# Second MLP product of an encoder layer: twenty block products over a 3 x 4 x 2 split in place of seven half products over a 2 x 2 x 2 split

## The reference, cut to what matters

```
h  = rms_norm(x, g_mlp) * (1.0 + scale2) + shift2     # (1536, 1024)
ff = square(relu(h @ w_ff1)) @ w_ff2                   # (1536,4096), then (1536,1024)
x  = x + gate2 * ff
y  = rms_norm(x, g_final)
```

## Time and profile before

| | |
|---|---|
| median of three runs | 1447.25 us (1443.58 to 1447.31) |
| span of the profiled execution | 1441.9 us |
| what lies around that span in the runs shown | 1.7 to 5.4 us, 5.35 to the median |
| TensorE busy | 1402.4 us, 97% of the span |
| VectorE, ScalarE, GpSimd busy | 809.9, 591.7, 479.5 us |
| first product, from its first matmul | 477.3 us |
| second product | 958.27 us to 1430.64 us |

### The profile page before, as it was taken

How to read it: one execution, slowest core, us unless ns; L and a number is a source line. 1 busy time by engine, 2 the same in 40 slices (tenths; PEclk the granted TensorE clock), 3 DMA queues, 4 the chain that set the end, 5 groups by cost and what they waited for, 6 DMA issues and landing times.

```text
span 1441.9 us, 18527 instructions
## 1 busy us (share of the span) xinstructions
PE 1402.4 (97%) x7594; PEld 1188.8 (82%) x7594; DVE 809.9 (56%) x756; ACT 591.7 (41%) x709; POOL 479.5 (33%) x275
## 2 busy tenths in 40 slices
PE   4999999999999989999999999999999999999997
PEld 2777777888888778888888888888888888888886
DVE  5967668794338994444453345352756433344575
ACT  6667888566135532232222222232232222433241
POOL 0011111137002655474545555432232222232131
PEclk9999999999999999999999999999999999999998
DMA  9344311203602234343334333479997444445542
GB/s 371 152 153 170 135 61 37 73 23 95 234 0 88 88 125 160 114 154 114 122 143 145 119 119 126 172 258 389 391 384 297 146 146 146 161 177 204 204 160 88
DMA packets 75411, 232.35 MB, mean 161 GB/s; under 512 B 5696, under 2 KB 9920, under 8 KB 66368
## 3 DMA queue, kind: packets, MB, share of 16 engines
q1 hardware_dynamic: 75328, 231.17, 43.5%
HBM read 166.14 MB, written 65.01 MB: 160 GB/s over the span
## 4 chain that ended last, share of the span: by engine, by line
PE 50%; issue 3%; POOL 1%; DVE 1%; ACT 0%; POOLq 0%; ACTq 0%
PE bank L981 17%; PE bank L982 17%; PE bank L983 16%; POOL w_lo L2339 1%; DVE x L2151 0%; DVE w_raw L2102 0%; POOL x L2361 0%; ACT hin_hi L1527 0%; ACT w_hi L1515 0%; DVE x L2123 0%; POOL w_s L2315 0%; PE bank L1038 0%; POOL w_lo L2331 0%; PE bank L1031 0%; POOLq L2369 0%
## 5 line engine op out<-in xcount | busy, mean ns | idle before, releaser
L981 PE MATMUL bank<-hin_hi,w_lo 128*128 128x512 f32 (+1 forms) x896 | 302.4, 337 | 1.4 <-DVE hin_lo L2107 1.4
L982 PE MATMUL bank<-hin_lo,w_hi 128*128 128x512 f32 (+1 forms) x896 | 301.7, 337 | 0.0
L983 PE MATMUL bank<-hin_hi,w_hi 128*128 128x512 f32 (+1 forms) x896 | 301.1, 336 | 0.0
L2107 DVE TENSOR_TENSOR hin_lo<-hin,hin_hi 128x3072 fp32r<-128x3072 f32 x28 | 140.9, 5031 | 209.1 <-ACT hin_hi L1527 209.1
L2339 POOL TENSOR_TENSOR w_lo<-w_raw,w_hi 128x2048 fp32r<-128x2048 f32 x28 | 129.6, 4628 | 329.9 <-ACT w_hi L1515 328.4
L981 PEld LDWEIGHTS bank<-hin_hi,w_lo 128*128 128x128 f32 x896 | 170.1, 190 | 20.4 <-issue 2.3
L983 PEld LDWEIGHTS bank<-hin_hi,w_hi 128*128 128x128 f32 x896 | 169.9, 190 | 18.0
L982 PEld LDWEIGHTS bank<-hin_lo,w_hi 128*128 128x128 f32 x896 | 170.1, 190 | 17.7 <-issue 0.2
L1515 ACT ACTIVATE w_hi<-w_raw 128x2048 fp32r<-128x2048 f32 x28 | 53.6, 1916 | 287.6 <-PE bank L983 181.7
L2331 POOL TENSOR_TENSOR w_lo<-w_raw,w_hi 128x512 fp32r<-128x512 f32 x51 | 73.5, 1441 | 208.5 <-ACT w_hi L1461 208.5
L1470 ACT ACTIVATE hid<-bank 128x768 f32<-128x768 f32 (+2 forms) x68 | 52.5, 772 | 162.7 <-PE bank L983 155.3
(11 more groups left out here) (273 smaller groups left out, 3171.1 us busy)
## 6 DMA issues: line engine op xcount, KB each, us to landing
hin<-hid_all SPq DMA_DIRECT2D x28, 1536.0 KB, 6.6
hid_all<-hid SPq DMA_DIRECT2D x105, 384.0 KB, 2.5
w_raw<-in_w_ff SPq DMA_DIRECT2D x36, 1024.0 KB, 8.9
w_raw<-in_w_ff SPq DMA_DIRECT2D x68, 256.0 KB, 2.9
mod_raw<-in_w_mod SPq DMA_DIRECT2D x16, 1024.0 KB, 5.1
x<-in_xT SPq DMA_DIRECT2D x5, 2048.0 KB, 14.1
w_sums<-w_raw SPq DMA_DIRECT2D x8, 1024.0 KB, 15.3
w_raw<-w_sums SPq DMA_DIRECT2D x8, 1024.0 KB, 10.1
```

Of the source, the lines that this page charges most:

```text
L981: pe.matmul(out, w_lo, v_hi, start=first, stop=False, skip_group_check=True)
L982: pe.matmul(out, w_hi, v_lo, start=False, stop=False, skip_group_check=True)
L983: return pe.matmul(out, w_hi, v_hi, start=False, stop=last, skip_group_check=True)
L2107: dve.tensor_tensor(hin_lo[n % 3][:].rearrange("p t n -> p (t n)"), hin[n % 3][:].rearrange("p t n -> p (t n)"), hin_hi[n % 3][:].rearrang ...
```

## The change

The second product is cut into 3 token blocks of 512, 4 inner blocks of 1024 and 2 column blocks of 512 (24 block products), and is computed as 20 products of sums of blocks. An inner block of 1024 has eight 128-wide tiles; the kernel goes through all 20 products for the first four tiles of each block (steps 0 to 19), then through all 20 for the other four (steps 20 to 39). A step has 4 banks x 4 tiles x 3 = 48 matmuls of 512 columns. Each product's result goes, with a sign, into one or more of six output blocks.

- The products alternate between two sets of four banks at first (indices 0 to 10 in `SEQ`); from index 11 on several follow one another on the same set: 17, 16, 13, 18, 15 on banks 0 to 3 and 12, 14, 11, 0 on banks 4 to 7 (the numbers are names of products).
- The splits into high and low are done in two pieces of 128 x 1024. The high parts have two buffers. In steps of `BY_BANK` a bank is finished before the next is begun, and both pieces are freed only at the step's end.
- VectorE makes 17 weight sums of 128 x 2048 in each half (34 in all) and 8 token sums of 128 x 2048 in each half; 13 additions of a whole output block (4 banks) from PSUM in the first half and 19 in the second. ScalarE copies 5 blocks from PSUM and one block within SBUF. `conv_block`, new, turns the accumulated sum into `gate * sum + x` for each of the six blocks in the second half; from then on additions carry the gate.
- The first product stores nine forms of 128 x 512 a job (fewer in the two parts of job 0): six combinations of 512 columns in place of four of 768. The four hidden blocks stay in one tensor `hidq`; ScalarE's copies into it wait for the combinations of the job before that read the same rows. Two blocks of job 0 are read back from DRAM before job 5 ends (`reload_rest`).
- The residual is loaded block by block late in the second half. Squares are added on GpSimd (`fin_adds`).

TensorE, order and waits (cut):

```
+SEQ = (7, 6, 10, 9, 5, 2, 8, 3, 4, 19, 1, 17, 16, 13, 18, 15, 12, 14, 11, 0)
+BY_BANK = (0,) + tuple(range(11, NP))
+SAME_NEXT = (11, 12, 13, 14, 16, 17, 18)
+        def bank_emptied(n, b):
+            if b % 2:
+                return
+            m = same_bank(n)
...
+            if added(m):
+                pe.wait_ge(ff2_add, adds_to(m, b // 2))
+        def product(n):
+            if n % NP in BY_BANK:
+                split_in(n, 0)
+                split_in(n, 1)
+                for b in range(4):
+                    bank_emptied(n, b)
+                    m = bank_part(n, b, range(GF))
...
+                    if n == NS - 2 and b == 1:
+                        fin_spread(0)
...
+            for p in range(2):
+                split_in(n, p)
+                for b in range(4):
+                    if p == 0:
+                        bank_emptied(n, b)
+                    m = bank_part(n, b, (2 * p, 2 * p + 1))
```

VectorE, order of the second product:

```
+        for s in range(NS):
+            h, i = half_of(s)
+            if i == 8:
+                token_add(h, "a14")
+            if s > 0 and added_later(s - 1):
+                block_adds(s - 1, 1)
+            if s + 1 < NS:
+                tok_split_lo(s + 1, 0)
+            if s > 0 and not added_later(s - 1):
+                block_adds(s - 1, 0)
+                block_adds(s - 1, 1)
+            if s + 1 < NS:
+                tok_split_lo(s + 1, 1)
+            for name in {1: ("b0a",), 2: ("b0b", "v"), 3: ("b2", "b3"), 5: ("b19",), 6: ("b4",), 7: ("b1",), 8: ("b17",),
+                         11: ("b13",), 13: ("v15", "b12"), 14: ("b14a", "b14b"), 16: ("b11",)}.get(i, ()):
+                weight_sum(h, name)
+            if s == NP - 1:
+                weight_sum(1, "u")
+                weight_sum(1, "b6")
+            if i in (8, 9, 10, 11, 12, 14, 16):
+                token_add(h, {8: "a1", 9: "a17", 10: "a16", 11: "a13", 12: "a18", 14: "a12", 16: "a11"}[i])
+            if h and i in CONV_AT:
+                conv_block(CONV_AT[i])
+            if s == NS - 2:
+                fin_diagonal(0)
+            if s < NS - 1 and added_later(s):
+                block_adds(s, 0)
+            if s == NS - 2:
+                for v, k in ((1, 0), (1, 1), (1, 2), (1, 3), (0, 0)):
+                    final_tile(0, v, k)
```

`block_adds(n, e)` adds banks 2e and 2e + 1 of product n to its output block or blocks; `added_later(s)` holds for `SAME_NEXT` and for step 19. GpSimd:

```
+        for s in range(NS):
+            if s + 1 < NS:
+                w2_split_lo(s + 1, 0)
+                w2_split_lo(s + 1, 1)
+            if s == NP + 16:
+                fin_adds(0, (1, 0), (1, 1))
+            elif s == NP + 18:
+                fin_adds(1, (2, 1), (2, 0))
+                fin_tiles(0, (1, 0))
```

SyncE, what it does at job 5, ahead of the next weights:

```
+        def reload_rest():
+            sp.wait_ge(hid_step, hid_at(REST, FR))
+            sp.wait_ge(st_hid[0], stored(0, REST))
+            sp.wait_ge(st_hid[1], stored(1, REST))
+            sp.wait_ge(st_keep, 16)
+            sp.dma_start(hidq[:, H11, 0:CH], keep_d).then_inc(ld_keep, 16)
+            sp.dma_start(hidq[:, H21, 0:CH], hid_d[0, 0, :, 0]).then_inc(ld_keep, 16)
```

More of the change, by code:

```diff
@@ L80 @@
[L80 to L92, removed]
+H11, H12, H21, H22 = range(4)
+G5, G2, G3, G15, GZ, G19 = range(6)
+G7, G6, GR, G9, G0, G4 = range(6)
+NST = 9
+FORMS = ("a00", 10, 5, 3, 2, 15, "a10", 19, "z", "a22", "a02", 7, "r", 6, 9, 8, 4, 0)
@@ new lines, in kind_of, with steps_of, hid_at, stores_of @@
+def kind_of(q):
+    return JOBS[q][0] % 8 // GF
+def steps_of(q):
+    both = (U2, C11, B11, C22, B22, C12, B12)
+    _, c0, c1 = JOBS[q]
+    if c0:
+        return both + (F19, FZ)
+    if c1 == CH:
+        return both + (F3, F5, F2, F15)
+    return both + ((F0, F4, F7, F6, F9, FR) if kind_of(q) else (F3, F19, F5, FZ, F2, F15))
+def hid_at(q, step):
+    return sum(len(steps_of(i)) for i in range(q)) + steps_of(q).index(step) + 1
+def stores_of(q):
+    _, c0, c1 = JOBS[q]
+    return (7, 8) if c0 else range(7) if c1 == CH else range(NST)
@@ new lines, in added, with copied, adds_to, copies_to @@
+def added(n):
+    h, i = half_of(n)
+    return ADDED[h].get(SEQ[i], ())
+def copied(n):
+    return COPIED.get(SEQ[n], ()) if n < NP else ()
+def adds_to(n, e):
+    return 2 * sum(len(added(m)) for m in range(n)) + (e + 1) * len(added(n))
+def copies_to(n):
+    return sum(len(copied(m)) for m in range(n + 1)) + (n >= SEQ.index(9))
+def same_bank(n):
+    side = SEQ[n % NP] in RIGHT
+    return next((m for m in range(n - 1, -1, -1) if (SEQ[m % NP] in RIGHT) == side and (added(m) or copied(m))), None)
@@ L306, in build_encoder @@
[L306 to L312, removed]
-    fin_acc = place("fin_acc", [P, HTOK], F32, hid_at + 12288)
@@ new lines, in _ @@
+        for n in range(NS):
+            if n == NS - 2:
+                fin_columns(0)
+            product(n)
+        pe.wait_ge(fin_last_added, 3)
+        for b in range(4):
+            pe.matmul(bank[3][:, 8 + b:9 + b], sq[0, 0][:, 0, b * P:(b + 1) * P], ones[:, 0:1], start=(b == 0),
+                      stop=False, skip_group_check=True)
+        pe.wait_ge(fin_last_sqd, 4)
+        for b in range(4):
+            m = pe.matmul(bank[3][:, 8 + b:9 + b], sq[0, 1][:, 3, b * P:(b + 1) * P], ones[:, 0:1], start=False,
+                          stop=True, skip_group_check=True)
@@ L2050, in out_of, with halves, split, pieces @@
                 return ps[:, 2 * CH * buf + c0:2 * CH * buf + c1]
-            slot, at = hid, NHID * q
+            def halves(lo_row):
+                return hidq[:, lo_row:lo_row + 2, CH:HTOK]
+            def split(i):
+                return form[i][:].rearrange("p (a b) -> p a b", a=2)
+            def pieces(row):
+                return hidq[:, row, 0:CH].rearrange("p (a b) -> p a b", a=2)
+            def stored_before(j):
+                if q:
+                    after(dve, st_hid[j], stored(j, q - 1))
+            h11, h12, h21, h22 = (hidq[:, i, 0:CH] for i in range(4))
             if step == U2:
@@ L2183, in _ @@
         token_lo(P5, 1)
-        for step in (B22, C12, B12, T1):
+        for step in (B22, C12, B12, F3):
             hid_out(0, step)
@@ L2194, in _ @@
         token_lo(P4, 1)
-        hid_out(0, T4)
+        for step in (F2, F15):
+            hid_out(0, step)
         for q in range(1, NJ):
```

1191 lines of the change are left out of this document (740 added, 451 removed), and 5 rows, old and new, of the table ADDED.

## The result

| | before | after |
|---|---|---|
| median | 1446.01 us (1443.58 to 1447.31, 4 runs) | 1502.31 us (1500.18 to 1504.36, 4 runs) |
| ratio, 95% interval | | 1.039 [1.037, 1.041] |
| span of the profiled execution | 1441.9 us | 1502.4 us |
| second product | 472.4 us | 509.9 us |
| behind its last matmul | 11.3 us | 15.8 us |

A forecast was written before the change was run, and what follows sets the result against it. It took TensorE's matmuls to bound the second product; 434.7 us of columns, 3 of small matmuls and 60 of waits made that stage 25.3 us longer. With +2 first product and +2.6 tail: 1477 us, range 1435 to 1500.

The forecast's parts named there:

- the walk: Second product, step by step through the engines' queues: TensorE waits 14 us in the first half, 46 in the second.
- 30.3 us of columns are saved: Second product: 1920 matmuls of 512 columns take 434.7 us in place of 465.0; a step shrinks to 10.87 us.
- VectorE and GpSimd hold each other: Second product: VectorE's SBUF work stands still during GpSimd's 4.8 us a step; instructions with one operand in PSUM aren't held.
- Waits of 60 us in the second product: New TensorE waits, mostly on VectorE: 60 us, at least 21 or 10 from below, about 85 from above.
- Indices 0 to 10: Second product, both halves: products change banks each time, so an addition has a whole step; waits taken as 0.
- The clock stays at full: Second product: no loss to half clock in the sum, since VectorE is behind and a slower step is partly covered.
- rival 3: Second product: clock falls after some six waits of 8 us or nearly, 16 us, 1493 us; chance 0.13, 0.05 with late loads.
- First product +2 us: First product: reload holding SyncE at job 5 ahead of job 6's weights costs 2 us, range 0 to 6.
- At the job boundary 0: First product: ScalarE's copy waits for the sum of H11 and H21, ready before the copy is due; 0 us.
- Tail +2.6: After the second product's last bank: 14 us in place of 11.3, so +2.6 us, range 0 to 5.
- Rival 1: Second product: splits fit, matmuls still bound, GpSimd's holds fall under PSUM additions or idle time; 10 us waits, 1427 us; chance 0.20.

The follow-up runs named there:

- e1: Changed kernel with GpSimd's low weight pieces of the second product written as zeros instead of subtracted, their product left out: 1458.97 us, ratio 1.009 to the kernel before.
- e9: Changed kernel with GpSimd writing zeros three times for each low weight piece of the second product, as long as the subtraction took: 1457.8 us, ratio 1.008.
- e10: e5 with the second product's low weight subtractions, all but the first step's, moved from GpSimd to VectorE, nothing left out: 1464.92 us, ratio 1.013.
- e2: Changed kernel with VectorE's addition of banks 0 and 1 moved ahead of the step's sums: 1484.64 us, ratio 1.027.
- e3: Changed kernel, first product: job 0's sum of H11 and H21 ahead of token sums, job 6's first two weight loads ahead of late stores and reload: 1496.26 us.
- e5: Changed kernel with the reorders of e2 and e3, and the first diagonal's product after bank 3 of step 38 instead of bank 1: 1477.29 us, ratio 1.022.
- e7: e5 with GpSimd writing zeros for the second product's low weight pieces as in e1: 1446.29 us, ratio 1.001.

## Why the prediction was right or wrong

The direction and the mechanism came out as forecast; the size did not. The time lies 25 us above the forecast of 1477 us. Two terms of the sum that stood at nothing or nearly so account for most of it. The half clock around TensorE's waits was put at 0 and cost some 16 us. The first product was put at +2 us, with 0 at its job boundary, and cost 13.5. The waits themselves were 9 us fewer than the walk had.

- *30.3 us of columns are saved: right.* A step without a wait takes 10.87 us; the one shown above is 10.90 us long.
- *VectorE and GpSimd hold each other: right, and it is the cause.* e1 and e9 show it without GpSimd's reads, e10 with the same subtraction on VectorE. What was read from the earlier trace rows before is what the new kernel does: 2.4 us where 1.2 would do. PSUM additions aren't held: 1.21 us. The held ones suffer in both directions. GpSimd's piece takes 2.97 us in the mean where I took 2.4. The sums of squares take 6.7 us where I took 4.6.
- *Waits of 60 us in the second product: near.* 51.3 us. First half 14 forecast, 15.9 measured, at the indices named (11: 4.9; 13: 2.8; 14: 2.3; 16: 2.9; 19: 3.0). Second half 46 forecast, 32.8 measured at the same indices (forecast in brackets): 11: 5.9 (4); 13: 9.6 (10.8); 14: 0.8 (8.4); 16: 3.4 (8); 17: 2.0 (2.7); 18: 9.5 (11); 19: 1.6 (1). Index 14 failed because I let each step begin afresh. A TensorE that has just stood for 9.6 us, and then runs at half clock, has given VectorE the time to catch up. e2 fits this: there index 13 waits for nothing, and index 14's step is 7.6 us too long. Indices 0 to 10: 2.7 us for 0, over both halves.
- *The clock stays at full: wrong, and the largest error of the sum.* I had it as rival 3 at 16 us and 18%, and left it out "partly covered". It cost 15.7 us in the second product, counted from TensorE's busy time at half clock, and at most 20.4 with all that the waits and the small matmuls leave over. Four waits of the second product and two of the first are above 4 us, and the granted clock fell during all six; it also fell with some of 2.0 to 3.4 us, and with others of 2.3 and 2.8 us it did not. The two stretches of one step show 2.9 us lost behind 4.9 us of wait. The rival's size was near (16 us in all; 2.7 us per wait against 2.0 in the mean of eight falls). Its condition was wrong: 8 us or longer lay far above the 1 us of idle time that had kept the clock in the earlier trace rows. I had no row between the two, though the trace had one: the wait of 2.5 us at about 506 us, with the clock at full behind it. The Trainium skill (TensorE: Matmul & The Clock Gate, What's actually happening) speaks of half clock after idling and of recovery under sustained work. The trace agrees, and a wait of 2.0 us was enough in one place. (The end of the trace before, which the prediction called on, shows the fall alone. The return is in the two stretches above, 0.79 and then 1.00.)
- *First product +2 us: wrong, +13.5 in the profile.* "At the job boundary 0" failed. I priced the copy's new wait from VectorE's work in a steady job, and not from job 0, where the token sums lie ahead of the form. At job 5 I counted GpSimd's wait for the weights. I missed that ScalarE has that split and TensorE's copy in one queue. e3 gives back 3.1 us of it in the profile (6.0 in the medians) with the two orders alone. In e5 the second product still starts 10 us later than in the kernel before (968.2 against 958.3 us).
- *Tail +2.6: +4.5.* Near enough; it was not taken apart further. The clock is at half at the end of both kernels (the earlier trace rows before; 0.50 over the last 4 us after).
- *Rival 1, the splits fit, 1427 us.* e1 and e9 are this case made true: GpSimd's subtraction costs VectorE nothing. The result is 1458 to 1459 us and not 1427, since the last steps, the first product and the clock keep some 31 us. With the three orders as well it is 1446, as the kernel before. So removing the holds alone, which is what this rival supposes, would not have brought a gain.

By size, the changed kernel's 56.3 us are: -30.3 columns, +49.9 new waits (51.3 less the 1.4 of before), +17.9 for the rest of the second product (23.9 us against 6.0 before; 15.7 of it is the clock), +13.5 first product, +4.5 tail, which is 55.5. Without GpSimd's reads 43 to 45 us of the 56.3 go (e1, e9), waits and clock together. This share depends on what else is mended. The three orders bring 25.0 us by themselves (e5), and behind them the same writes bring 31.0 (e7). The two sets together give back the whole 56.0 us, though each measured alone would promise 68 or more.

What stays open: how the 26 us of the last five steps could be had. In e7 16.4 of them are waits for VectorE. GpSimd's sums of squares explain 5.7 us of its lateness there; what the rest comes from was not shown. Moving those sums to another engine was not tried. None of the ten kernels measured after the change, some of which leave work out, beats the one before.

## What to carry to other kernels

When a stage gets shorter, work out for each engine what it must do in the new step, and count each GpSimd instruction that reads SBUF two times over: once on GpSimd, and once as time in which VectorE's instructions with two SBUF operands stand. If a low piece costs GpSimd 2.97 us and VectorE 1.45 us of holding, let VectorE do it in 1.22 us. Here this gave 12.4 us (e10 against e5).

Where TensorE must wait for a result, put that result first in the queue of the engine that makes it. This helps only where that engine has slack over the following steps. Add 2 to 3 us to every wait of some 4 us or more for the clock behind it: here all six such waits lost it.

## What the runs showed of the hardware

- A GpSimd memset of 1024 fp32 columns takes 0.956 us and does not hold VectorE in any way that the traces show. Three in a row, 2.98 us, leave the median of VectorE's token piece at 1224 ns (e9). The subtraction of the same length, which reads two operands, gives 2586 ns.
- Three sums of squares on GpSimd in 8.9 us stretch four VectorE instructions from 2.73 to 8.47 us (e7).
- The granted clock fell to half in the middle of dense work, at about 304 us, in two of the twelve profiled executions, with no wait of TensorE over 0.7 us in that stretch. Beside the changed kernel it was e10:

```profile
300.00:313.00 13.00, 12.45 (x67) 11.27 (x67) 13.00 (x18) 10.06 (x18) 3.59 (x3) 0.74 0.01 2
```
